# Scoring the heads of the second block's attention one at a time instead of in interleaved pairs

## The chip, the core and the metric

The kernel runs on one core of a Trainium2 chip. The metric is the device time of one execution in microseconds (us); several executions are timed and the median is taken. TensorE (PE in the profile) multiplies matrices, VectorE (DVE) and ScalarE (ACT) work on rows, GpSimd (POOL) and SyncE (SP) mostly issue DMAs.

## The reference

Two model blocks of two layers each on 512 tokens of width 1024, in float32. The change touches the attention of the second block. Layer 0 there is windowed attention with a sink, layer 1 global attention with normed queries and keys; both also look at 256 context tokens, and in layer 0 the context tokens attend to themselves.

```python
def _mixer_window(q, k, v, kc, vc, sink, cos, sin):
...
    def block(i):
...
        s_lat = jnp.einsum('bqhgd,bkhd->bhgqk', qb, kb).astype(jnp.float32)
        s_lat = jnp.where(mask, s_lat, NEG_INF_2)
        s_ctx = jnp.einsum('bqhgd,bkhd->bhgqk', qpb, kc).astype(jnp.float32)
        p_lat, p_ctx = _joint_softmax(s_lat, s_ctx, sink)
        return (jnp.einsum('bhgqk,bkhd->bqhgd', p_lat.astype(v.dtype), vb)
                + jnp.einsum('bhgqk,bkhd->bqhgd', p_ctx.astype(vc.dtype), vc))
```

There are 16 query heads of width 64, and blocks of 128 queries (four for the latent tokens, two for the context tokens). After attention come an output projection and a mixture of 32 experts, then the next layer.

## The kernel before

A plan of steps is written first (`make_plan`), and each engine then walks the same list of steps and issues its own part of each one in that order. Nothing reorders the steps later, so the place of a step in the plan is its place in every engine's queue.

The unit of attention work is one head (or, for context queries, two heads of different groups) for 128 queries. A unit has four steps:

- **scores** (PE, L1162): queries times keys into PSUM tile `SC`, which has two buffers (unit index modulo 2). A window or global head has two products: the "plain" one with the 256 context keys, and the "rotated" one with the latent keys (256 or 384 of them in the window layer, 512 in the global layer). Each contracts over only 64 rows. For an even head the plain product sits in the lower 64 rows of the array and the rotated one in the upper 64; for an odd head it is the other way round (`pieces`, L876). Window heads add one or two masks by a 128-row bf16 product with the identity (`SC<-KB`). The buffer must have been freed by the exp of the unit two before (`sc_free`). VectorE then takes a row minimum over the scores.
- **exp** (ACT, L1582): the exponentials from `SC` into `PR`; frees the `SC` buffer.
- **turn** (PE, L1567 is its ACT half): 128x128 transposes of `PR` into PSUM tile `TR` (two banks, four blocks in each), which ACT copies to `PT`. The profile's line is L1190.
- **weigh** (PE, L1192; its products are L1200): `PT` times the values into `PJ`; after four heads VectorE divides by the sums.

`attend_pair` (L236) orders these for two units at a time: scores of i and i+1, turn of i-2, exp of i, weigh of i-3, exp of i+1, turn of i-1, weigh of i-2. `o_turn` (L1308, products L1085) turns a finished block of 128 queries for the output projection. For a pair of window heads the masks of both come behind the four products of both. The loop at L474 to L476 calls `attend_pair` for 80 units in layer 0 (64 window heads, 16 context units) and 64 in layer 1; the first pair is begun ahead of the last projection tile (L452).

The attention of the first block (`attend`, L257) is already written head by head: scores of i, turn of i-2, exp of i, weigh of i-3.

Of the kernel before, what the change touches and what calls it, by code (L numbers as in the profile page):

```python
# [128 lines left out]
class Counting:  # L129
# [5 lines left out]
    def add(self, sem, n):  # L135
        self.count[sem.name] = self.count.get(sem.name, 0) + n
        self.latest = (sem, self.count[sem.name])
# [34 lines left out]
def make_plan(until=99):  # L172
# [24 lines left out]
    def add(kind, **kw):  # L197
        s = Step(kind=kind, tr_before=n["tr"] - len(kw.get("tr", ())), **kw)
        steps.append(s)
        users = kw.get("w")  # L200
        if users is not None and kw.get("last", True):

            for u, use in zip(users if isinstance(users, list) else [users], kw["pj"] if isinstance(kw["pj"], list) else [kw["pj"]]):
                u.done = use + 1
        return s

    def begin_unit(u, first):
        u.sc = take("sc")[0]
        u.index = attend.count
        attend.count += 1  # L210
        u.two_before = units_before[-2] if len(units_before) >= 2 else None
        units_before.append(u)
        n["mixed"] += u.kind == "diff"
        u.mixed = n["mixed"]
        u.first = first
        if u.slot == 0:
            attend.batch += 1
            n["sinks"] += u.kind in ("window", "ctx")
        u.batch, u.sinks = attend.batch, n["sinks"]
        s = add("scores", u=u)  # L220
        u.needs = s.tr_before

    def turn_unit(u):
        u.tr = take("tr", -(-u.blocks // 4))
        add("turn", u=u)

    def weigh_unit(u):
        if u.slot == 0:
            attend.pj = take("pj")[0]
        u.pj = attend.pj  # L230
        if not u.full:
            n["part"] += 1
        u.part = n["part"]
        add("weigh", u=u)

    def attend_pair(unit_list, i, after):  # L236


        m = len(unit_list)
        if i < m:  # L240
            begin_unit(unit_list[i], i == 0)
            begin_unit(unit_list[i + 1], False)
        if 2 <= i < m + 2:
            turn_unit(unit_list[i - 2])
        if i < m:
            add("exp", u=unit_list[i])
        if i - 5 in after:
            after[i - 5]()
        if 4 <= i < m + 4:
            weigh_unit(unit_list[i - 3])  # L250
        if i < m:
            add("exp", u=unit_list[i + 1])
        if 2 <= i < m + 2:
            turn_unit(unit_list[i - 1])
            weigh_unit(unit_list[i - 2])

    def attend(unit_list, extra=None, after=None):  # L257

# [37 lines left out]
    for l in range(DEPTH):  # L296
# [29 lines left out]
        for ci, name in enumerate(names):  # L326
            w = weight("w_in", l=l, cols=CHUNKS[name])
            for t in range(XT_TILES):
# [7 lines left out]
                if ci >= 2:  # L336
# [6 lines left out]
                    for tt in (1, 2, 3):  # L343
                        if topk_left[tt] and tt < ci - 1:
                            k = min(4 if ci < 5 else 2, topk_left[tt])
# [13 lines left out]
        unit_list = []  # L359
# [48 lines left out]
    for l in range(DEPTH):  # L408
# [9 lines left out]
        unit_list, last_unit = [], []  # L418
# [20 lines left out]
        after = {k: oturn(t) for t, k in enumerate(last_unit)}  # L439
# [99 lines left out]
        for k, (what, e) in enumerate(order):  # L539
# [3 lines left out]
            u = Step(kind=what, l=l, e=e, index=base + k, slot=slot, loads=slot_loads[slot], prev=prev_use)  # L543
# [121 lines left out]
def build(nc, ins, out, until=99, debug=None):  # L665
# [6 lines left out]
    with ctx:  # L672
# [161 lines left out]
        sc_full, sc_free = sem("sc_full"), sem("sc_free")  # L834
# [41 lines left out]
        def pieces(u):  # L876
            t = u.t
            q = slice(t * P, (t + 1) * P)
            lo, hi = slice(0, HD), slice(HD, P)
            if u.kind in ("window", "global"):  # L880
                g, at_, k = u.h // 4, u.lat[0] * P, len(u.lat) * P
                plain, rotated = (hi, lo) if u.h % 2 else (lo, hi)
                found = [(256, CTX, QS[plain, u.h, q], KCTX[plain, g, :]),
                         (512, k, QS[rotated, u.h, q], KROT[rotated, g, at_:at_ + k])]
                if plain == hi:
                    found.reverse()
                for k, kb in enumerate(u.lat):
                    if u.kind == "window" and kb != t:
                        found.append((512 + k * P, P, identB, belowB if kb < t else aboveB))
                return found  # L890
            ext = u.keys * P if u.kind != "ctx" else CTX
            found = []
            for m, half in enumerate((lo, hi)):
                if u.kind == "ctx":
                    g = u.h // 4
                    qc = slice((t - XT_TILES) * P, (t - XT_TILES + 1) * P)
                    found.append((512 * m, ext, QCTX[half, (g // 2) * 4 + u.h % 4, qc], KCTX[half, g + m, :]))
                elif u.kind == "diff":
                    found.append((512 * m, ext, blk[half, u.h, q], blk[half, 4 + u.h, 0:ext]))
                elif u.kind == "dsa":  # L900
                    found.append((512 * m, ext, blk[half, 14 + u.h // 2, q], blk[half, 13, 0:ext]))
                else:
                    found.append((512 * m, ext, blk[:, 16 + u.h + m, q], blk[:, 20 + u.h + m, 0:ext]))
            for m in range(2):
                if u.kind == "dsa" and t:
                    found.append((512 * m, ext, identB, SELt[t]))
                elif u.kind != "ctx":
                    found.append((512 * m + t * P, P, identB, aboveB))
            return found
# [156 lines left out]
        def _(pe):  # L1066
# [34 lines left out]
                           YR[g][0:CAP, h * 512:(h + 1) * 512], start=g == 0, stop=g == 1)  # L1101
                return x

            scored_units = {}

            def score(u, ps, a, b):

                for k, (col, n, lhsT, rhs) in list(enumerate(ps))[a:b]:
                    bank = col // 512
                    m = mm(SC[:, u.sc % 2, col:col + n], lhsT, rhs, start=all(p[0] // 512 != bank for p in ps[:k]),  # L1110
                           stop=all(p[0] // 512 != bank for p in ps[k + 1:]), skip_group_check=True)
                return m
# [6 lines left out]
            for s in steps:  # L1119
                if s.kind == "open":  # L1120
                    turn_open(s.t, s.tr)
                elif s.kind == "project":
# [6 lines left out]
                    for c in range(DC):  # L1129
                        if c == DC // 2 and s.inner:  # L1130
                            turn_open(s.t + 1, s.inner)
                        m = mm(bank[:, 0:n], XT1[:, c, s.t * P:(s.t + 1) * P], w[:, c, 0:n], start=c == 0,  # L1132
                               stop=c == DC - 1)
                    m.then_inc(pj_full, 1)
                elif s.kind == "stage_turn":
# [3 lines left out]
                    for k in range(s.count):  # L1139
                        m = turn(bank[0:s.rows, k * P:(k + 1) * P], STG[:, base + k * s.rows:base + (k + 1) * s.rows],  # L1140
                                 identF)
                    m.then_inc(tr_full, 1)
                elif s.kind == "forget":
# [4 lines left out]
                    for t in range(XT_TILES):  # L1148
                        for j in range(t + 1):
                            m = mm(bank[:, 4 * t:4 * t + 4], triF if j == t else onesF, FT[3][:, 4 * j:4 * j + 4],  # L1150
                                   start=j == 0, stop=j == t)
# [9 lines left out]
                    x.then_inc(sc_full, 1)  # L1161
                elif s.kind == "scores":  # L1162
                    u = s.u
                    scored_units[u.index] = u
                    if u.first:
                        pe.wait_ge(tr_free, u.needs)
                    if u.kind == "dsa" and u.t:
# [1 line left out]
                    if u.sc >= 2:  # L1169
                        pe.wait_ge(sc_free, u.sc - 1)  # L1170
                    ps = pieces(u)
                    if u.kind != "window":
                        score(u, ps, 0, len(ps)).then_inc(sc_full, 1)
                        continue

                    score(u, ps, 0, 2)
                    if u.h % 2:
                        for a in (scored_units[u.index - 1], u):
                            score(a, pieces(a), 2, 2 + len(a.lat) - 1).then_inc(sc_full, 1)
                elif s.kind == "turn":  # L1180
                    u = s.u
                    if u.kind == "diff":
# [4 lines left out]
                    for k, use in enumerate(u.tr):  # L1187
                        bank = tr_slot(use)
                        for b, src in enumerate(blocks[4 * k:4 * k + 4]):
                            m = turn(bank[:, b * P:(b + 1) * P], src, identF)  # L1190
                        m.then_inc(tr_full, 1)
                elif s.kind == "weigh":  # L1192
                    u = s.u
# [3 lines left out]
                    for col, n, vs in weighed(u):  # L1197
                        for b, v in enumerate(vs):
                            for r in range(0, P, HALF_ROWS):
                                m = mm(bank[r:r + HALF_ROWS, col:col + n], PT[:, o + r:o + r + HALF_ROWS], v, start=b == 0,  # L1200
                                       stop=b == len(vs) - 1)
# [5 lines left out]
                elif s.kind == "ada":  # L1207
# [5 lines left out]
                    for c in range(DC):  # L1213
                        for g in range(4):
                            m = mm(bank[32 * g:32 * g + 2, 0:P], SCT[:, 2 * c:2 * c + 2], w[:, c, g * P:(g + 1) * P],
                                   start=c == 0, stop=c == DC - 1)
# [18 lines left out]
                elif s.kind == "scored":  # L1235
# [6 lines left out]
                    for c in range(4):  # L1242
                        for h in range(2):
                            k = 4 * h + c
                            m = mm(SC[64 * h:64 * h + ROUTER, 0, 0:P], RWT[:, k * ROUTER:(k + 1) * ROUTER],
                                   xt2(s.t)[:, k, :], start=c == 0, stop=c == 3)
# [12 lines left out]
                elif s.kind == "ranks":  # L1259
                    pe.wait_ge(mask_ready, s.index + 1)  # L1260
                    pe.wait_ge(rank_read, s.index)
                    for j in range(s.t + 1):
                        m = mm(SC[:, 1, 0:EXPERTS], beforeB if j == s.t else onesB, MASKB[:, j * EXPERTS:(j + 1) * EXPERTS],
                               start=j == 0, stop=j == s.t)
                    m.then_inc(rank_full, 1)
                    if s.t == s.tiles - 1:
                        pe.wait_ge(rank_read, s.index + 1)
                        for j in range(s.tiles):
                            m = mm(SC[:, 1, 0:EXPERTS], onesB, MASKB[:, j * EXPERTS:(j + 1) * EXPERTS], start=j == 0,
                                   stop=j == s.t)  # L1270
                        m.then_inc(count_full, 1)
                elif s.kind == "slots":
                    pe.wait_ge(slot_ready, s.index + 1)
                    for k in range(2):
                        m = mm(SC[0:CAP, 1, 512:512 + EXPERTS], SLOT[s.index % 2][:, k, :], OWNT[:, s.t, k, :],  # L1275
                               start=s.t + k == 0, stop=s.t == s.tiles - 1 and k == 1)
                    m.then_inc(slots_done, 1)
                elif s.kind == "fin_turn":
                    f = s.f
                    pe.wait_ge(fin_done, f.q)  # L1280
                    k = f.fin % 2
# [1567 lines left out]
```

## Time and profile before

| what | value |
|---|---|
| median of 3 runs | 2901.52 us (2897.41 to 2903.01) |
| profiled execution, its own time | 2897.14 us |
| its span | 2895.3 us |
| mean granted TensorE clock | 0.988 |
| TensorE busy (matmul) | 2785.2 us, 96% of the span |
| VectorE, ScalarE, GpSimd busy | 1115.7, 760.8 and 235.4 us |
| DMA | 636.91 MB, mean 220 GB/s |
| the chain that ended last | PE 20% of the span, DVE 1%, the rest 0% |

All times below are microseconds from the start of the span. The second block's attention lies at about 1016 to 1196 (layer 0) and 2015 to 2195 (layer 1). TensorE's matmuls are pipelined, so the duration of one says less than the distance from one start to the next. A group's line, such as L1110 for scores, is the line in the code above.

### The profile page before, as it was taken

Reading aid. Unit: us, or ns where it says so; the run is one execution under the profiler, and the core shown is the slowest. Engines: PE = TensorE matmul, PEld = TensorE weight load, DVE = VectorE, ACT = ScalarE, POOL = GpSimd, SP = SyncE. Lnnn points to the kernel's source line nnn. Section 1 sums busy time; section 2 is a strip of 40 time slices with the busy share of each in tenths; the row PEclk is TensorE's granted clock in tenths of the full one; section 3 lists DMA queues with packets and bytes.
Section 4 is the critical chain, followed back from the end, with each engine's and each line's share of the span. In section 5 each row is a group of like instructions: output and inputs, shape, how many; then the busy total and the mean of one; then the engine's idle time right before and its main releaser. Section 6 shows DMA issues by size and latency. Waiting matters only on the chain. (4 is left out here: it accounts for less than half of the span.)

```text
span 2895.3 us, 64923 instructions
## 1 busy us (share of the span) xinstructions
PE 2785.2 (96%) x27109; PEld 1650.7 (57%) x27109; DVE 1115.7 (39%) x2681; ACT 760.8 (26%) x1599; POOL 235.4 (8%) x400
## 2 busy tenths in 40 slices
PE   8999999999989999999999999989999999999996
PEld 4544655444644467546666666634675566666663
DVE  2572643672643255453221212273443522222224
ACT  1211521102631167411111111153773111111111
POOL 3000011000020000011000000120000100110001
PEclk9999999999989999999999999999999999999998
DMA  7213733114734000347999999861003699999993
GB/s 270 80 58 111 271 119 114 59 58 148 261 103 145 29 2 2 139 174 269 399 401 401 398 401 402 340 244 67 2 2 132 261 396 398 402 403 399 400 398 142
DMA packets 149741, 636.91 MB, mean 220 GB/s; under 512 B 14336, under 2 KB 18528, under 8 KB 133200
## 3 DMA queue, kind: packets, MB, share of 16 engines
q1 hardware_dynamic: 114624, 517.59, 46.2%
q0 software_dynamic: 34960, 117.16, 11.7%
q8 instruction: 106, 1.74, 0.2%
q14 instruction: 51, 0.42, 0.0%
HBM read 582.70 MB, written 52.00 MB: 219 GB/s over the span
## 5 line engine op out<-in xcount | busy, mean ns | idle before, releaser
L1132 PE MATMUL PJ<-WR,XT 128*128 128x512 f32 (+2 forms) x1152 | 475.4, 569 | 5.4 <-ACT XT L140 2.8
L140 ACT ACTIVATE PT<-TR 128x512 f32<-128x512 f32 (+3 forms) x384 | 177.8, 493 | 866.3 <-PE TR L1361 730.5
L1132 PEld LDWEIGHTS PJ<-WR,XT 128*128 128x128 f32 x1152 | 215.6, 191 | 243.8 <-issue 215.9
L140 DVE TENSOR_TENSOR PR<-G 128x384 f32<-128x384 f32 x64 | 35.7, 559 | 736.2 <-ACT G L140 735.8
L1090 PE MATMUL PJ<-WR,XT 128*128 128x512 f32 x576 | 259.0, 606 | 1.8 <-ACT XT L140 1.4
L1341 PE MATMUL SC<-QK,XT 128*64 128x256 f32 x2112 | 242.5, 383 | 0.0
L140 DVE TENSOR_REDUCE SM<-SC 128x1 f32<-128x768 f32 (+6 forms) x208 | 173.7, 835 | 172.5 <-PE SC L1110 167.3
L1292 PE MATMUL PJ<-WR,XT 128*128 128x512 f32 x512 | 225.7, 593 | 1.0 <-issue 1.0
L1341 PE MATMUL SC<-WR,XT 128*64 128x256 f32 x1984 | 226.2, 381 | 0.0
L1341 PEld LDWEIGHTS SC<-QK,XT 128*64 128x64 f32 x2112 | 149.4, 138 | 85.4 <-issue 14.5
L140 ACT ACTIVATE PR<-SC,SM 128x256 f32<-128x256 f32 (+5 forms) x288 | 187.6, 669 | 31.5 <-DVE SM L140 15.3
L140 ACT ACTIVATE XT<-TR 128x384 f32<-128x384 f32 (+1 forms) x204 | 99.4, 526 | 338.8 <-PE TR L1327 241.4
L1090 PEld LDWEIGHTS PJ<-WR,XT 128*128 128x128 f32 x576 | 109.9, 195 | 132.6 <-issue 130.4
L1341 PEld LDWEIGHTS SC<-WR,XT 128*64 128x64 f32 x1984 | 139.8, 137 | 79.6 <-issue 12.3
L1200 PE MATMUL PJ<-V,PT 128*64 128x65 f32 (+1 forms) x3904 | 167.4, 231 | 1.4 <-ACT PT L140 1.4
L1110 PE MATMUL SC<-QK 64*128 64x512 f32 (+7 forms) x512 | 155.0, 512 | 1.9 <-ACT PR L140 1.7
L1200 PEld LDWEIGHTS PJ<-V,PT 128*64 128x64 f32 x3904 | 135.8, 137 | 36.0 <-issue 32.6
L1292 PEld LDWEIGHTS PJ<-WR,XT 128*128 128x128 f32 x512 | 94.6, 190 | 108.3 <-issue 108.3
L140 ACT ACTIVATE QK<-TR 128x512 f32<-128x512 f32 (+4 forms) x108 | 59.2, 563 | 367.9 <-PE TR L1140 272.7
L1190 PE MATMUL TR<-KF,PR 128*128 128x128 f32 x976 | 148.0, 281 | 7.3 <-DVE PR L140 4.0
L1351 PE MATMUL SC<-QK,XT 128*32 128x128 f32 x4224 | 127.9, 273 | 0.0
L140 DVE TENSOR_TENSOR XT<-PJ,BC 32x256 f32<-32x256 f32 (+1 forms) x192 | 98.0, 510 | 74.1 <-PE PJ L1374 56.2
(253 smaller groups left out, 3147.5 us busy)
## 6 DMA issues: line engine op xcount, KB each, us to landing
QK<-in_w_gate_dram SPq DMA_DIRECT2D x34, 2048.0 KB, 9.4
WR<-in_w_down_dram SPq DMA_DIRECT2D x34, 2048.0 KB, 15.6
QK<-in_w_up_dram SPq DMA_DIRECT2D x32, 2048.0 KB, 13.2
WR<-in_w_up_dram SPq DMA_DIRECT2D x32, 2048.0 KB, 14.3
WR<-in_w_gate_dram SPq DMA_DIRECT2D x30, 2048.0 KB, 9.5
QK<-in_w_down_dram SPq DMA_DIRECT2D x30, 2048.0 KB, 15.8
WR<-in_w_ada_dram SPq DMA_DIRECT2D x24, 2048.0 KB, 8.5
WR<-in_w_in_dram SPq DMA_DIRECT2D x14, 2048.0 KB, 8.0
```

Source lines behind the costliest of these rows:

```text
L140: return lambda *a, **k: Signal(make(*a, **k), self)
L1090: m = mm(dst[:, 0:n], rows[:, c, :], w[:, c, 0:n], start=c == 0, stop=c == DC - 1)
L1110: m = mm(SC[:, u.sc % 2, col:col + n], lhsT, rhs, start=all(p[0] // 512 != bank for p in ps[:k]), stop=all(p[0] // 512 != bank for p in ps ...
L1132: m = mm(bank[:, 0:n], XT1[:, c, s.t * P:(s.t + 1) * P], w[:, c, 0:n], start=c == 0, stop=c == DC - 1)
L1190: m = turn(bank[:, b * P:(b + 1) * P], src, identF)
L1200: m = mm(bank[r:r + HALF_ROWS, col:col + n], PT[:, o + r:o + r + HALF_ROWS], v, start=b == 0, stop=b == len(vs) - 1)
L1292: m = mm(bank, rows[:, c, :], w[:, c, :], start=c == 0, stop=c == DC - 1)
L1341: mm(bank[CAP_A * h:CAP_A * (h + 1), k * 512:k * 512 + 256], XET[par][:, c, 0:CAP_A], w[:, c, 256 * h:256 * (h + 1)], start=c == 0, stop=c ...
L1351: x = mm(bank[CAP_B * q:CAP_B * (q + 1), k * 512 + 256:k * 512 + 384], XET[par][:, c, CAP_A:CAP], w[:, c, P * q:P * (q + 1)], start=c == 0 ...
```

## The change

`attend_pair` now orders its two units one after the other, with the same four steps in the order that the first block uses: scores of k, turn of k-2, exp of k, weigh of k-3, and then the same for k+1. On TensorE, a window head's products and masks are issued together, where before the masks of a pair came behind the products of both heads. The diff is whole:

```diff
-        if i < m:
-            begin_unit(unit_list[i], i == 0)
-            begin_unit(unit_list[i + 1], False)
-        if 2 <= i < m + 2:
-            turn_unit(unit_list[i - 2])
-        if i < m:
-            add("exp", u=unit_list[i])
-        if i - 5 in after:
-            after[i - 5]()
-        if 4 <= i < m + 4:
-            weigh_unit(unit_list[i - 3])
-        if i < m:
-            add("exp", u=unit_list[i + 1])
-        if 2 <= i < m + 2:
-            turn_unit(unit_list[i - 1])
-            weigh_unit(unit_list[i - 2])
+        for k in (i, i + 1):
+            if k < m:
+                begin_unit(unit_list[k], k == 0)
+            if 2 <= k < m + 2:
+                turn_unit(unit_list[k - 2])
+            if k < m:
+                add("exp", u=unit_list[k])
+            if k - 5 in after:
+                after[k - 5]()
+            if 3 <= k < m + 3:
+                weigh_unit(unit_list[k - 3])
...
-            scored_units = {}
-
...
-                    scored_units[u.index] = u
...
-                    if u.kind != "window":
-                        score(u, ps, 0, len(ps)).then_inc(sc_full, 1)
-                        continue
-
-                    score(u, ps, 0, 2)
-                    if u.h % 2:
-                        for a in (scored_units[u.index - 1], u):
-                            score(a, pieces(a), 2, 2 + len(a.lat) - 1).then_inc(sc_full, 1)
+                    score(u, ps, 0, len(ps)).then_inc(sc_full, 1)
```

The number of instructions of each kind is the same; only their order changes, on PE, ACT and DVE. GpSimd's and SyncE's rows are the same as before.

TensorE in the global layer (layer 1), one pair of heads, before. `SC<-V,QK` is the plain product, `SC<-QK` the rotated one, `TR<-KF,PR` the turn of one head, `PJ<-V,PT` its weighing:

```order
L1110 MATMUL SC<-V,QK 128x256
L1110 MATMUL SC<-QK 128x512 x2
L1110 MATMUL SC<-V,QK 128x256
L1190 MATMUL TR<-KF,PR 128x128 x6
L1200 MATMUL PJ<-V,PT 64x65 x12
L1190 MATMUL TR<-KF,PR 128x128 x6
L1200 MATMUL PJ<-V,PT 64x65 x12
```

The same in the changed kernel:

```order
L1103 MATMUL SC<-V,QK 128x256
L1103 MATMUL SC<-QK 128x512
L1175 MATMUL TR<-KF,PR 128x128 x6
L1185 MATMUL PJ<-V,PT 64x65 x12
L1103 MATMUL SC<-QK 128x512
L1103 MATMUL SC<-V,QK 128x256
L1175 MATMUL TR<-KF,PR 128x128 x6
L1185 MATMUL PJ<-V,PT 64x65 x12
```

The second head's two products have moved from beside the first head's to behind the first turn and weighing.

TensorE in the window layer, a pair of heads of the second or third query tile, before:

```order
L1110 MATMUL SC<-V,QK 128x256
L1110 MATMUL SC<-QK 128x384 x2
L1110 MATMUL SC<-V,QK 128x256
L1110 MATMUL SC<-KB 128x128 x4
L1190 MATMUL TR<-KF,PR 128x128 x5
L1200 MATMUL PJ<-V,PT 64x65 x10
L1190 MATMUL TR<-KF,PR 128x128 x5
L1200 MATMUL PJ<-V,PT 64x65 x10
```

The same, changed, for its first head:

```order
L1103 MATMUL SC<-V,QK 128x256
L1103 MATMUL SC<-QK 128x384
L1103 MATMUL SC<-KB 128x128 x2
```

The four masks of the pair have been split, two behind each head's own products.

ScalarE in the global layer, the exps (`PR<-SC,SM`) and the copies of turned blocks (`PT<-TR`, 512 and 256 wide for one head), before:

```order
L140 ACTIVATE PR<-SC,SM 128x768 x2
L140 ACTIVATE PT<-TR 128x512
L140 ACTIVATE PT<-TR 128x256
L140 ACTIVATE PT<-TR 128x512
L140 ACTIVATE PT<-TR 128x256
L140 ACTIVATE PR<-SC,SM 128x768 x2
```

Changed:

```order
L140 ACTIVATE PT<-TR 128x512
L140 ACTIVATE PT<-TR 128x256
L140 ACTIVATE PR<-SC,SM 128x768
L140 ACTIVATE PT<-TR 128x512
L140 ACTIVATE PT<-TR 128x256
L140 ACTIVATE PR<-SC,SM 128x768
```

The copy of the second head's turned blocks now stands ahead of that pair's second exp.

## Rows read from the trace of the kernel before

**Rows 1.** Windows: stretch, length, busy by engine (instructions), clock, DMA share, GB/s.
```profile
1016.30:1190.00 173.70, 168.04 (x2168) 121.33 (x2168) 96.08 (x265) 121.59 (x240) 0.00 (x0) 1.00 0.01 2
2037.00:2042.00 5.00, 4.36 (x14) 1.74 (x14) 1.06 (x5) 4.12 (x7) 0.00 (x0) 0.70 0.00 0
2053.00:2190.00 137.00, 134.32 (x1863) 100.49 (x1861) 68.83 (x136) 104.29 (x169) 0.00 (x0) 1.00 0.01 2
```

**Rows 2.** Timeline (start, us, what), PE: one global pair, scores, turn, next pair.
```profile
2072.54 0.48 PE L1110 MATMUL SC<-V,QK 64*128 64x256 f32 x1
...
2074.08 0.87 PE L1190 MATMUL TR<-KF,PR 128*128 128x128 f32 x6
...
2077.39 0.48 PE L1110 MATMUL SC<-V,QK 64*128 64x256 f32 x1
```

**Rows 3.** Timeline, PE: single heads of the first block, scores, masks, turn.
```profile
305.26 0.70 PE L1110 MATMUL SC<-QK 64*128 64x256 f32 x4
305.90 0.28 PE L1110 MATMUL SC<-KB 128*128 128x128 bf16 x2
...
321.84 0.92 PE L1110 MATMUL SC<-QK 64*128 64x384 f32 x4
322.69 0.29 PE L1110 MATMUL SC<-KB 128*128 128x128 bf16 x2
...
348.61 1.13 PE L1110 MATMUL SC<-QK 64*128 64x512 f32 x4
349.67 0.29 PE L1110 MATMUL SC<-KB 128*128 128x128 bf16 x2
349.79 0.61 PE L1190 MATMUL TR<-KF,PR 128*128 128x128 f32 x4
```

**Rows 4.** Timeline, ACT and DVE in the pair of Rows 2: minimum, copy, exps.
```profile
2073.80 0.96 DVE L140 TENSOR_REDUCE SM<-SC 128x1 f32<-128x768 f32 x1 [2.51 <-PE SC L1110]
...
2074.86 0.87 ACT L140 ACTIVATE PT<-TR 128x512 f32<-128x512 f32 x2 [0.98 <-PE TR L1190]
...
2075.76 2.06 ACT L140 ACTIVATE PR<-SC,SM 128x768 f32<-128x768 f32 x2
```

**Rows 5.** Timeline, PE: one window pair of the second query tile, and the next.
```profile
1071.39 0.48 PE L1110 MATMUL SC<-V,QK 64*128 64x256 f32 x1
...
1072.90 0.72 PE L1190 MATMUL TR<-KF,PR 128*128 128x128 f32 x5
...
1073.55 0.80 PE L1200 MATMUL PJ<-V,PT 128*64 128x65 f32 x20
...
1074.37 0.74 PE L1190 MATMUL TR<-KF,PR 128*128 128x128 f32 x5
...
1075.77 0.48 PE L1110 MATMUL SC<-V,QK 64*128 64x256 f32 x1
```

**Rows 6.** Timeline, PE: a window pair of the first query tile, and the next.
```profile
1032.11 0.48 PE L1110 MATMUL SC<-V,QK 64*128 64x256 f32 x1
...
1033.47 0.60 PE L1190 MATMUL TR<-KF,PR 128*128 128x128 f32 x4
...
1035.82 0.48 PE L1110 MATMUL SC<-V,QK 64*128 64x256 f32 x1
```

**Rows 7.** Timeline, PE: a pair of context units, and the next.
```profile
1177.87 1.51 PE L1110 MATMUL SC<-V,QK 64*128 64x256 f32 x8
1179.32 0.66 PE L1190 MATMUL TR<-KF,PR 128*128 128x128 f32 x4
...
1181.72 1.51 PE L1110 MATMUL SC<-V,QK 64*128 64x256 f32 x8
```

**Rows 8.** Timeline, PE: waits (in brackets) at layer 1's start and end.
```profile
2037.50 0.48 PE L1110 MATMUL SC<-V,QK 64*128 64x256 f32 x1 [2.73 <-ACT PR L140]
...
2190.43 0.84 PE L1190 MATMUL TR<-KF,PR 128*128 128x128 f32 x6 [1.14 <-ACT PT L140]
```

**Rows 9.** Timeline, PE: sixteen passes of projection, 512 wide over all 128 rows.
```profile
1017.49 7.08 PE L1292 MATMUL PJ<-WR,XT 128*128 128x512 f32 x16
```

## The prediction, written before the changed kernel ran

> **What bounds the kernel now.** I read three views in this order. The windows first [rows 1]: in the global layer's attention TensorE is busy for 134.3 of 137.0 us, at a granted clock of 1.00, and ScalarE for 104.3; in the window layer it is 168.0 of 173.7, ScalarE 121.6. The DMA columns beside them say 2 GB/s, so no transfer runs under either stretch that could hide a longer or use a shorter attention. The time of these stages is what TensorE's instruction stream needs, plus the few waits in it. Then the timeline of TensorE, to see what its stream consists of: I take distances from one start to the next, since matmuls overlap. A global pair [rows 2] takes 2072.54 to 2077.39 = 4.85 us, of which the scores of both heads take 1.54 (to the first turn) and two turns and two weighings the other 3.31. Last the same view in the first block [rows 3], which orders heads one by one already, and so shows what a head scored alone costs.
>
> **What the rows say of a head scored alone.** A head's two products sit in different halves of the array and run at the same time. With both 256 wide, the scores last 305.90 - 305.26 = 0.64 us until the masks; with both 384 wide 0.85; with both 512 wide 1.06 [rows 3]. That is 0.21 for each further 128 columns of both, above some 0.22 that a group of scores costs once. A pair of global heads has 512 + 256 on either half, since the second head has its halves swapped: 0.22 + 6 x 0.21 = 1.48, and 1.54 is what is seen. Alone, a global head has 512 on one half and 256 on the other. If the longer half decides, that is 1.06 and two of them 2.12; if the halves shared one stream, the mean width of 384 would count, 0.85, and two 1.70. The trace has no row of unequal halves alone. What decides for me: a pass of 512 over all 128 rows takes 7.08 / 16 = 0.44 [rows 9], and the step from two 256-wide passes to two 512-wide ones in both halves at once costs 1.06 - 0.64 = 0.42, so 0.42 for 2 x 256 more columns on either side. A half in company is as fast as the full array by itself, so the companion takes nothing away and its absence gives nothing back. I take the longer half: 1.06. Upper end 1.10, since a 128-row float32 turn and not a bf16 mask follows here.
>
> The interleaving of before thus was a packing: the short product of one head ran beside the long one of the next. The change takes this away wherever the two products differ in width, and everywhere pays the 0.22 of a group twice per pair instead of once.
>
> **The change part by part**, all on TensorE's stream; counts are of pairs.
>
> (A) Global layer, steady part: 27 pairs start between 2053.19 and 2184.37, 23 with scores of 1.54 as in rows 2, and four of 1.49 that do not wait for an exp. Two solo heads are 2.12. 23 x 0.58 + 4 x 0.63 = +15.9. Turns and weighings are the same instructions (3.31), and the period should be 5.43.
>
> (B) Window layer, second and third tile: 16 pairs. Today 1.51 for scores with four masks [rows 5]. Alone: 0.85 for a 384-wide longer half, and 0.12 for two masks (349.79 - 349.67 [rows 3]) = 0.97, twice 1.94. 16 x 0.43 = +6.9; two of these pairs wait today, 1.68 and 1.99, which goes: -0.7. The first weighing lasts 0.82 there, with the turn ahead 1.47 in all, against 1.40 for the second turn and weighing: the next turn waits for its bank. With scores between, that goes: 16 x 0.07 = -1.1. Together +5.1, a period of 4.38 becoming 4.7.
>
> (C) Window layer, first and last tile: 16 pairs with both products 256 wide. Alone 0.64 + 0.06 for one mask = 0.70, twice 1.40. Today 1.36 [rows 6] where the second head waits for an exp, which is most pairs, and 1.19 where it does not; the mean of the 16 is 1.33. +1.1, and minus some 1.7 for waits before scores, before the first weighing and after a tile's o_turn: -0.6.
>
> (D) Context units: 8 pairs, equal widths. Today 1.45 [rows 7], alone 0.67 each (0.64 and 0.03 for the turn that follows; between 0.64 and the 0.72 that would leave it even). A period of 3.85 becomes 3.74; with two o_turns whose waits shrink by 0.2 each: -1.3.
>
> (E) Ends. In layer 1 a turn waits 1.14 for a bank because ACT does two exps before it copies [rows 8]; with the copy between them it goes: -1.1, and the like in layer 0: -1.1. At layer 1's start scores wait 2.73 for an exp that is late because the last projection tile and its rope sit on VectorE and ScalarE in front of it [rows 8]. I estimate from the order of the steps there that the exp will be ready 0.5 to 1 us sooner, and that a turn further on, which like that of 2190.43 waits about 1.14 for a bank, no longer does: -2.2 in all, the least certain term. The pair begun ahead of the last projection becomes 0.6 longer: +0.6. Sum -3.8.
>
> **Does the new order add a wait?** The longest loop is scores, minimum, exp, buffer free. In the global layer [rows 4]: the minimum takes 0.96, a pair of exps 2.06, so one about 1.0, the copy 0.87 beginning 0.78 after its turn's start. Counted from the turn in slot k: copy done at 1.65, exp k from 1.7 to 2.7; the next turn comes at 2.7, the scores that need this buffer at 2 x 2.72 - 1.06 = 4.4. Slack 1.7. ScalarE's copy and exp are 1.9 of a period of 2.7. The weighing needs a copy that is a whole slot old. VectorE's division after each fourth head now stands between two minima, and queues behind it the minimum of the next head; it needs about 1 us and the scores beside it last 1.06. I cost all this at nothing; its cover is the slack just counted.
>
> **A rule of the Trainium skill, weighed.** TensorE's stream changes between 64-row products, full 128-row ones and 64-column ones: today five such changes per pair, from now on six. What the sixth costs stands in the rows as part of the 0.22 and of the turns' 0.04 after it, and is counted. "TensorEngine Tiling (Array Packing)", Key Properties, of the Trainium skill says that changing the tiling mode drains the engine, and "TensorE: Matmul & The Clock Gate" of the Trainium skill, Single matmul latency, puts the drain at about 175 ns. By it, as an estimate, 72 pairs might pay up to 0.07 more than counted, +5 us; the steps between rows show about 0.1 after a group of scores and I stay with them.
>
> **Sum.** 15.9 + 5.1 - 0.6 - 1.3 - 3.8 = +15.3 us. Against the profiled execution's own 2897.14 (span 2895.3 and 1.8 around it) this is 2912.4. That execution lies 4.4 below the median of 2901.52, within the spread of 2897.41 to 2903.01; against the median it is 2916.8. Everything behind attention starts later by the same amount: the expert weights' first transfers are issued as the attention ends.
>
> **Rivals.**
> 1. *Halves share a stream* (solo global head 0.85, not 1.06): A becomes 27 x 0.17 = +4.5, B 16 x 0.22 less 1.8 = +1.7, the pair ahead -0.4 and the rest as before, in sum about +0.1: 2901.6, no change. Against it are rows 9 and 3 side by side, as above. 6%.
> 2. *Faster*: a head scored alone costs no more than half a pair, because the array takes up the next head's loads during the weighing ahead of it and the 0.22 vanishes with the longer half's surplus. Then A = 0, B = -1.8, C = -1.7, D and E as counted less 0.6: -9.2, so 2892. The sign turns when A and B together lose 15.3 us over their 43 pairs, 0.36 per pair or 0.18 per head: at a solo global head below 0.88. The first block's heads [rows 3], which have this very order, show 1.06. 3%.
> 3. *A new wait in each slot*: ScalarE comes late for the turn's bank or the exp, say 0.3 in each of the 54 steady global heads, +16: 2933. It needs ScalarE to be 1 us later than rows 4 make it. 5%.
> 4. *Part of the waits stays or more goes*: TensorE's clock fell to 0.70 in the 5 us after the wait of 2.73 [rows 1, 8]. If the wait shrinks enough for the clock to stay at 1.00, up to 2.4 us more are won at that place: 2914.4. If none of E comes, 2920.6. Both are in the forecast's own range.
>
> **How the numbers follow.** The forecast with its range of 2909 to 2923 has 86%; the bounds are E with or without, 1.10 in place of 1.06 (+2.2 in A) and 2 to 3 us of spread between medians. The range of 8 in 10 is 2908 to 2924. A difference of 0.2%, 5.8 us, is about what a measurement of this kernel can tell from no change. Slower by more: the forecast nearly whole and rival 3, 91%. Within: rival 1 and the forecast's lower tail, 6%. Faster by more: rival 2, 3%.
>
> **What would show it.** In the changed profile: global slots of 2.72 us (turn to turn) with scores of 1.06 from their first start to the turn; window slots of 2.36 in the middle tiles and 1.86 in the outer ones; no wait of TensorE for an exp in steady state, so that TensorE's matmul columns stay at 98% or more while the stage is longer; the global stage 16 us longer and the window and context stage 1 to 3. The prediction is wrong if the solo scores of unequal halves last under 0.95, if bracketed waits stand in each slot, or if the time behind attention shrinks by what attention grows.

## The result and the profile after

The changed kernel takes 2919.04 us (median, 2918.15 to 2919.48, 4 runs) beside 2899.47 for the kernel before (2896.93 to 2903.01, 4 runs). The ratio is 1.0061, 95% interval 1.0047 to 1.0076: slower by 0.5 to 0.8%. The forecast was 2916.8 us, with a range of 2908 to 2924.

The two attention stages, each from the start of its first scores to the start of its last `o_turn`, carry most of it. In the windows view (stretch, length, then busy time and instructions of PE, PEld, DVE, ACT, POOL, then granted clock, DMA share, GB/s), the kernel before:

```profile
1016.30:1196.32 180.02, 172.13 (x2242) 124.43 (x2241) 98.76 (x278) 125.00 (x247) 0.00 (x0) 1.00 0.01 3
2015.48:2195.52 180.04, 170.51 (x2234) 123.79 (x2233) 87.32 (x176) 132.04 (x212) 0.00 (x0) 0.99 0.01 2
```

and the changed one:

```profile
1018.06:1200.28 182.22, 177.78 (x2241) 119.78 (x2241) 98.74 (x278) 125.06 (x247) 0.00 (x0) 1.00 0.01 3
2024.23:2216.98 192.75, 186.83 (x2233) 118.44 (x2233) 87.34 (x176) 132.11 (x212) 0.00 (x0) 0.99 0.01 2
```

Layer 0 grew by 2.20 us, layer 1 by 12.71. VectorE and ScalarE did the same work in the same busy time; TensorE's busy time grew by 5.65 and 16.32 us with the same instructions. More of its time is a product running in one half of the array with nothing in the other.

This is a pair of global heads of the changed kernel, on PE, which answers to [rows 2]:

```profile
2099.89 0.48 PE L1103 MATMUL SC<-V,QK 64*128 64x256 f32 x1
2099.90 0.69 PE L1103 MATMUL SC<-QK 64*128 64x512 f32 x1
2100.21 0.38 PE L1103 MATMUL SC<-V,QK 64*128 64x256 f32 x1
2100.43 0.59 PE L1103 MATMUL SC<-QK 64*128 64x512 f32 x1
2100.95 0.87 PE L1175 MATMUL TR<-KF,PR 128*128 128x128 f32 x6
2101.76 0.92 PE L1185 MATMUL PJ<-V,PT 128*64 128x65 f32 x24
2102.61 0.69 PE L1103 MATMUL SC<-QK 64*128 64x512 f32 x1
...
2103.66 0.88 PE L1175 MATMUL TR<-KF,PR 128*128 128x128 f32 x6
2104.46 0.92 PE L1185 MATMUL PJ<-V,PT 128*64 128x65 f32 x24
2105.31 0.48 PE L1103 MATMUL SC<-V,QK 64*128 64x256 f32 x1
```

Scores last 1.06 and 1.05 from their first start to the turn, where the pair had 1.54; the pair's period is 5.42, where it was 4.85. Both products start at once. The short one issues its second pass at 2100.21, the long one at 2100.43, and from there the long one runs on without a companion. For the wide window heads, which answer to [rows 5]:

```profile
1080.59 0.59 PE L1103 MATMUL SC<-QK 64*128 64x384 f32 x1
...
1081.43 0.28 PE L1103 MATMUL SC<-KB 128*128 128x128 bf16 x2
1081.56 0.72 PE L1175 MATMUL TR<-KF,PR 128*128 128x128 f32 x5
1082.20 0.80 PE L1185 MATMUL PJ<-V,PT 128*64 128x65 f32 x20
1082.93 0.48 PE L1103 MATMUL SC<-V,QK 64*128 64x256 f32 x1
```

0.97 for scores and masks, and 2.34 for a head, so 4.69 for two against 4.38. For the context units, which answer to [rows 7], a head takes 1.84, two 3.68 against 3.85.

```profile
1163.28 0.70 PE L1103 MATMUL SC<-V,QK 64*128 64x256 f32 x4
1163.91 0.66 PE L1175 MATMUL TR<-KF,PR 128*128 128x128 f32 x4
1164.50 0.69 PE L1185 MATMUL PJ<-V,PT 128*64 128x65 f32 x16
1165.12 0.70 PE L1103 MATMUL SC<-V,QK 64*128 64x256 f32 x4
```

ScalarE and VectorE are in time. Counted from the turn at 2100.95, the copy begins 0.78 later and the exp ends 2.67 later (2102.63 + 0.99), which is 1.7 before the scores that need its buffer, at 2105.31:

```profile
2101.16 0.96 DVE L140 TENSOR_REDUCE SM<-SC 128x1 f32<-128x768 f32 x1 [1.57 <-PE SC L1103]
2101.73 0.87 ACT L140 ACTIVATE PT<-TR 128x512 f32<-128x512 f32 x2 [0.82 <-PE TR L1175]
...
2102.63 0.99 ACT L140 ACTIVATE PR<-SC,SM 128x768 f32<-128x768 f32 x1
```

At layer 1's start and end, which answer to [rows 8], the wait for the late exp is 2.15 where it was 2.73, and the turn near the end, which had waited 1.14, has no bracket any more:

```profile
2045.87 0.48 PE L1103 MATMUL SC<-V,QK 64*128 64x256 f32 x1 [2.15 <-ACT PR L140]
```
```profile
2211.71 0.87 PE L1175 MATMUL TR<-KF,PR 128*128 128x128 f32 x6
2212.51 0.92 PE L1185 MATMUL PJ<-V,PT 128*64 128x65 f32 x24
2213.55 0.85 PE L1175 MATMUL TR<-KF,PR 128*128 128x128 f32 x6
```

The stages make 14.9 us. Of the 22.4 us between the two profiled spans (2917.7 and 2895.3), 7.5 lie outside them; of the 19.6 between the medians, 4.7. The experiments ask what these are.

### The profile page after: what moved, and what is told of

Same layout as the page of the kernel before. It is cut to its first block and busy times, and to the rows that moved or that the text cites. A ratio compares the mean times of both kernels' runs of the same rounds, so it can differ in the third digit from the quotient of the medians.

```text
span 2917.7 us, 64835 instructions
## 1 busy us (share of the span) xinstructions
PE 2813.1 (96%) x27105; PEld 1643.2 (56%) x27109; DVE 1115.6 (38%) x2681; ACT 761.4 (26%) x1599; POOL 235.7 (8%) x400
## 5 line engine op out<-in xcount | busy, mean ns | idle before, releaser
L1103 PE MATMUL SC<-QK 64*128 64x512 f32 (+7 forms) x512 | 183.3, 519 | 1.4 <-ACT PR L140 1.4
L1175 PEld LDWEIGHTS TR<-KF,PR 128*128 128x128 f32 x976 | 104.3, 141 | 60.8 <-ACT PR L140 37.0
```

## The experiments

All ratios are to runs of the kernel before on the same chip, in the same job. The theory: the longer half of the array decides how long a head's scores last, and a pair was cheap since one head's short product ran beside the other's long one. The rivals: the halves share one stream; the order of waits, and not the packing, made the pair cheap; part of the loss lies outside attention.

### E1, the short product twice, heads one by one

```diff
+                    if u.kind == "global":
+                        ps = [p for p in ps for _ in range(1 + (p[0] == 256))]
```

(with start and stop set for each product of a global head, so that the second one overwrites the first).

> The changed kernel, but each global head multiplies its short product (plain, 256 wide) twice into the same place; 64 heads do 256 columns more on one half of the array. Theory (the longer half of the array alone sets a head's scores, and the short one runs beside it for nothing): both halves now carry 512, scores stay at 1.06 us, layer 1 and the whole stay within 1 us of the changed kernel (about +19 us against before). Rival (the halves share a stream, the sum of widths counts): 0.21 us more per head, 64 x 0.21 = +13 us, about +33 against before.

2913.58 us, ratio 1.0054 (1.0032 to 1.0076). Two heads on PE:

```profile
2100.61 0.69 PE L1103 MATMUL SC<-QK 64*128 64x512 f32 x1
2100.62 0.70 PE L1103 MATMUL SC<-V,QK 64*128 64x256 f32 x2
2101.14 0.59 PE L1103 MATMUL SC<-QK 64*128 64x512 f32 x1
2101.15 0.59 PE L1103 MATMUL SC<-V,QK 64*128 64x256 f32 x2
2101.68 0.87 PE L1177 MATMUL TR<-KF,PR 128*128 128x128 f32 x6
...
2103.33 0.48 PE L1103 MATMUL SC<-V,QK 64*128 64x256 f32 x1
```

Four passes of 256 beside two of 512 take 1.07 where two beside two took 1.05 to 1.06. Layer 1's stage is 193.7 us against 192.75. 64 more products cost 0.9 us, not 13, and 0.44 of it falls on the one pair that still stands side by side, ahead of the last projection (9.87 us to the next scores, where it was 9.43). A head scored alone has that much room in its shorter half. The halves do not share a stream.

### E2, the same in the pairs of before

The same two lines in the kernel before.

> The kernel before, pairs as they were, with the short product of each global head multiplied twice. Theory: in a pair each half carries 256 + 512 now and 256 x 2 + 512 then, so the pair's scores grow from 1.54 to about 1.90 (0.22 + 8 x 0.21), 32 pairs x 0.37 to 0.42 = +12 to +13 us against before. Rival (a pair was cheap because of the order of waits and not because the long product ran beside the other head's short one): under +4 us.

2909.39 us, ratio 1.0038 (1.0026 to 1.0049). One pair:

```profile
2101.55 0.48 PE L1110 MATMUL SC<-V,QK 64*128 64x256 f32 x1
2101.57 0.69 PE L1110 MATMUL SC<-QK 64*128 64x512 f32 x1
...
2103.48 0.88 PE L1192 MATMUL TR<-KF,PR 128*128 128x128 f32 x6
```

Scores 1.93 instead of 1.54, layer 1's stage 191.7 instead of 180.0, so +11.6 us for the same 64 products that cost 0.9 in E1. And with both halves full, heads one by one (193.7) are only 2.0 us behind pairs (191.7), where with unequal halves they are 12.7 behind. So of the 12.7 us some 10.7 are the empty half beside the long product. The other 2.0 are the group of scores that is begun twice, 5.0 over the 26 steady pairs (146.5 against 141.5), less 2.1 at the layer's start and 0.8 at its end, where waits go.

### E3 and E4, the new order in one layer alone

`attend_pair` takes the new order where `u.l == 0` (E3) or `u.l == 1` (E4), and the old one elsewhere; the masks of window heads go with it.

> Head by head in the window layer (layer 0) only, pairs in the global layer. Theory from the two traces: the stage of layer 0 from its first scores to its last o_turn grows by 2.2 us (180.0 to 182.2), layer 1 stays at 180.0; in all +2 us against before, or +2 to +9 if what the changed kernel lost outside both stages (about 7 us between the two profiles) hangs on layer 0. Rival (that outside part is only variation between executions): stages as said and the outside part the same as before, within 3 us.

> Head by head in the global layer (layer 1) only. Theory: the stage of layer 1 grows by 12.7 us (180.0 to 192.8), layer 0 stays at 180.0; in all +13 us against before. Rival (the outside part follows the longer layer 1): +17 to +20 us.

E3: 2900.43 us, ratio 1.0013 (1.0002 to 1.0023); stages 182.22 and 180.07. E4: 2909.49 us, ratio 1.0043 (1.0033 to 1.0054); stages 180.03 and 194.29. The two layers add up but for 1.5 us, by which layer 1 of E4 lies above that of the changed kernel. This excess lies at its start, and by these rows the clock accounts for it. In the changed kernel the granted clock falls right behind the wait of 2.15, to a mean of 0.66 over five microseconds, and the next scores still wait 0.89 for an exp, so that part of what the slow clock costs would have been a wait in any case. In E4 it is 1.00 behind the first wait (2.14), TensorE then waits 0.67 and 1.73, and only behind that does it fall, where no wait follows that could hide it:

```profile
2047.03:2052.03 5.00, 5.00 (x38) 3.26 (x38) 1.12 (x2) 3.73 (x6) 0.00 (x0) 0.66 0.01 3
```

The same piece of layer 1, from the start of its second pair of heads to that of its sixth, lasts 26.58 us in the changed kernel, 28.12 in E4, and 26.61 in E1, where the clock does not fall at all. The outside part is 2535.4 and 2532.6 us: it follows neither layer.

### E5, the changed kernel again

> The changed kernel as it is, a second time. In its first profile 7.5 us more than in the profile of before lay outside the two attention stages (2542.7 against 2535.2), while four other kernels with one or both stages changed show 2532.6 to 2537.1 there. Theory (the outside part is variation between executions and chips): stages 182.2 and 192 to 194 again, outside 2532 to 2540, ratio to before about 1.0051 (+15 us). Rival (the changed order brings something about outside the stages): outside 2542 again, ratio 1.0065 or more.

2918.54 us (2912.08 to 2921.47), before 2901.71 (2893.39 to 2906.91), ratio 1.0057 (1.0039 to 1.0075). Stages 182.22 and 192.74, outside 2538.5. The stages repeat to 0.01 us. The outside part does not: over the two first profiles and the eight of the experiments it is 2532.6 to 2542.7 us, and the kernel before alone spreads over 13 us in one job. The 4.7 us between the first medians are within that; the ratio is a little above what the stages give (1.0051), and 16.8 us against 14.9 is no difference that these runs can settle.

### E6, the pairs of before with each head's masks behind its own products

```diff
-                    if u.kind != "window":
+                    if True:
```

> The order of before (pairs), but a window head's masks are issued right behind its own products and not behind those of both heads. Theory (a full 128-row mask between the heads ends the packing): in the 16 pairs with 384-wide products the scores grow from 1.51 to 1.94 us, +6.9; in the others (256 wide) from 1.19 to 1.40 where nothing waits and hardly at all where the second head waits for an exp, +1; layer 0's stage about 187 to 188 us against 180.0, more than the 182.2 of the changed kernel because the waits of the pair order stay; layer 1 stays at 180; +7 us. Rival (masks run between for their own 0.06 us each): under +1 us.

2915.35 us, ratio 1.0048 (1.0030 to 1.0065). One pair of the second tile:

```profile
1075.08 0.48 PE L1110 MATMUL SC<-V,QK 64*128 64x256 f32 x1
...
1075.92 0.28 PE L1110 MATMUL SC<-KB 128*128 128x128 bf16 x2
1076.14 0.59 PE L1110 MATMUL SC<-QK 64*128 64x384 f32 x1
...
1076.98 0.28 PE L1110 MATMUL SC<-KB 128*128 128x128 bf16 x2
1077.10 0.72 PE L1190 MATMUL TR<-KF,PR 128*128 128x128 f32 x5
```

Nothing in TensorE's queue moved but two masks of 0.06 us, and the pair's scores grew from 1.51 to 2.02. The second head's products start only behind both masks, 0.22 after the first of them, and have the array to themselves. Layer 0's stage is 189.7 us, 9.7 more than before, and 2 more than I had expected: a return from masks to half-array products costs 0.09 in each pair (1.49 against twice 0.70, 2.03 against twice 0.97), which heads one by one do not pay, since a weighing stands in front. It is shown with this that ending the packing costs layer 0 that much when nothing else moves; the changed kernel's +2.2 is this loss, less the 0.09 per pair and less the waits that the old order had. Layer 1, which the edit does not touch, was expected to stay at 180 and took 181.4. The difference is again at its start (29.66 us for the piece that takes 28.28 before), where the granted clock falls twice in this run, to 0.67 behind a wait of 2.74 and to 0.71 over the five microseconds from 2059.14; before it falls once.

### E7, pairs, but the copy of turned blocks ahead of the second exp

```diff
-        if i < m:
-            add("exp", u=unit_list[i + 1])
         if 2 <= i < m + 2:
             turn_unit(unit_list[i - 1])
+        if i < m:
+            add("exp", u=unit_list[i + 1])
+        if 2 <= i < m + 2:
             weigh_unit(unit_list[i - 2])
```

> Pairs scored side by side as before, but on ScalarE the copy of the second head's turned blocks stands ahead of the pair's second exp, as in the changed kernel. The packing stays. Theory (this order suits only heads that are scored apart; the scores of the next pair's second head now wait for a later exp): the second head's scores wait about 0.5 us in each global pair and 0.4 in each window pair, layer 1 +10 to +15, layer 0 +8 to +12, in all +18 to +27 us. Rival (the order of copies and exps does not matter in steady state and only helps the ends): -1 to -2 us.

2946.94 us, ratio 1.0160 (1.0137 to 1.0183), stages 202.2 and 202.3: +22 in each, twice what I had expected. The pair on PE and ACT:

```profile
2099.97 0.69 PE L1111 MATMUL SC<-QK 64*128 64x512 f32 x1 [0.26 <-ACT PR L140]
...
2102.68 0.87 PE L1191 MATMUL TR<-KF,PR 128*128 128x128 f32 x6
2102.71 0.99 ACT L140 ACTIVATE PR<-SC,SM 128x768 f32<-128x768 f32 x1
...
2103.78 0.87 ACT L140 ACTIVATE PT<-TR 128x512 f32<-128x512 f32 x2
...
2104.34 0.69 PE L1111 MATMUL SC<-QK 64*128 64x512 f32 x1
...
2104.69 0.99 ACT L140 ACTIVATE PR<-SC,SM 128x768 f32<-128x768 f32 x1
...
2105.73 0.69 PE L1111 MATMUL SC<-QK 64*128 64x512 f32 x1 [0.27 <-ACT PR L140]
```

It closes a loop: the second head's scores (2099.97), two turns, the copy held back by the first exp (2103.78), the second exp (to 2105.68), and the buffer for the next pair's second head: 5.76 us per pair. I had only set the later exp against the old period, and had not followed its delay around. I had also expected the packing to stay, and it does not: the first head's scores begin at 2104.34 and the second's only at 2105.73, 1.39 later, when the first's are done (a head alone takes 1.06). The pair's scores last 2.45 instead of 1.54, and these 0.91 are the whole growth of the period (5.76 against 4.85); only some 0.3 of them are the wait itself. The order of waits thus matters very much to pairs, and of the two the old one is right for them; it is not what the change lost by, for in the changed kernel nothing waits for an exp in steady state.

### E8, each order where it is cheaper

```diff
+    def single(u, i, m):
+
+        return u.kind == "ctx" or u.kind == "window" and u.t == 0 or u.kind == "global" and i < 10
```

Units that it names go head by head, the others as pairs; in the last pair of all the second exp stands behind the copy.

> Each order where it is cheaper: head by head for the first window tile, for the context units and for the first ten global heads; pairs for the wide window tiles and the other global heads; in the last global pair the copy ahead of the second exp. From the segments of the two traces: layer 0 -0.2 (first tile), -1.4 (context units), -0.8 (end) = 177.6 us against 180.0; layer 1 -1.7 (start), -1.0 (end) = 177.3 against 180.0; in all -5 us, ratio 0.9982. Rival (the seams between the orders cost what the parts gain): -2 to +1 us.

2898.93 us, ratio 0.9994 (0.9983 to 1.0004): no difference that can be measured in the whole. In the trace the stages are shorter by 1.7 and 2.1:

```profile
1021.65:1199.99 178.34, 173.25 (x2241) 123.67 (x2241) 98.80 (x278) 125.01 (x247) 0.00 (x0) 1.00 0.01 3
2018.45:2196.37 177.92, 171.54 (x2234) 123.82 (x2233) 87.36 (x176) 132.04 (x212) 0.00 (x0) 0.99 0.01 2
```

3.8 of the 5 us expected; the rest went at the seams, where the first pair behind single heads has scores of 2.12 instead of 1.68, and at the end of layer 1, where one weighing still lasts 1.20 and the turn after it waits 0.28.

## Why the prediction was right, point by point

| term | forecast | in the trace |
|---|---|---|
| A, global layer, 27 pairs | +15.9 | +14.9 for 26 pairs, and 0.6 for the last: +15.4 |
| B, window tiles 2 and 3 | +5.1 | +4.4 (73.72 to 78.10) |
| C, window tiles 1 and 4 | -0.6 | 0.0 (+0.3, -0.5 and +0.2) |
| D, context units | -1.3 | -1.4 (33.74 to 32.38) |
| E, ends and layer 1's start | -3.8 | -3.6 |
| sum | +15.3 | +14.9 |

**The disputed step**, whether the longer half or the sum of both decides, was settled as forecast: 1.06 and 1.05 in the trace, and E1 and E2 show the mechanism by itself. The reasoning from [rows 3] and [rows 9], that a companion takes nothing away, held. Rival 1 falls with E1, rival 2 with the scores themselves. Rival 3 falls with the waits view: in the steady part of layer 1 TensorE waits for ScalarE three times 0.6 us, ahead of the `o_turn`s, in both kernels, and not in each slot. This is the changed one, 2060 to 2210:

```profile
PE TR L1080 <- ACT PT L140: 1.9, 3, 0.6
```

**A** was 0.5 high. Half of it is the first weighing after an `o_turn`, which fell from 0.94 to 0.85 three times and which I had counted as unchanged; the other half is that the second head of a pair takes 1.05 and not 1.06. **B** was 0.7 high. A turn and weighing of a wide head now last 1.37 to 1.38 us, where I had counted 1.40: the second turn of a pair, which stood behind a weighing, took 0.67 to the weighing after it, and behind a mask it takes 0.64 or 0.65. Over 32 heads that is the 0.7. **C** had the gain 0.6 too large. The wait of 0.41 for an exp in the first tile, which I had counted as going, is still there as 0.45:

```profile
1044.15 0.48 PE L1110 MATMUL SC<-V,QK 64*128 64x256 f32 x1 [0.41 <-ACT PR L140]
```
```profile
1046.03 0.48 PE L1103 MATMUL SC<-V,QK 64*128 64x256 f32 x1 [0.45 <-ACT PR L140]
```

The first pair of the layer, whose products the first head's mask now parts, costs 0.3 and not 0.2.

**E** is right in sum by errors that cancel. The pair ahead of the last projection was to cost 0.6 and cost nothing. The new loop puts no turn between units 0 and 1 of layer 1, so they still stand side by side and pack; from their scores to the next scores it is 9.43 us in both kernels. That this term and the overstated savings cancel is luck. Layer 1's start gave 1.7 of the 2.2 forecast (0.6 of the late exp, and the 1.14 of a turn), its end 1.0 of 1.1, layer 0's end 0.8 of 1.1.

**Rival 4** put a price of up to 2.4 us on the fall of the clock at layer 1's start. In the changed kernel the clock was not spared: it is 0.74 in the five microseconds from 2045, as it was 0.70 in those from 2037 before [rows 1], and 0.66 in both when counted from the end of the wait.

```profile
2045.00:2050.00 5.00, 4.13 (x36) 2.89 (x38) 1.47 (x4) 4.65 (x7) 0.00 (x0) 0.74 0.00 0
```

In E1 it was spared, behind a wait as long:

```profile
2043.73 0.48 PE L1103 MATMUL SC<-V,QK 64*128 64x256 f32 x1 [2.12 <-ACT PR L140]
```
```profile
2043.73:2048.73 5.00, 4.35 (x47) 3.31 (x48) 1.38 (x5) 4.34 (x7) 0.00 (x0) 1.00 0.00 0
```

And nothing was won by it: that piece of the layer takes 26.61 us in E1 and 26.58 in the changed kernel, since the faster TensorE waits 0.65 for a copy and 1.73 for the next exp instead of 0.89. No run bears out the 2.4.

**The rule of the skill.** The further 5 us did not come: the steady parts A and B stayed below their forecasts, which went by [rows 3]. E6 gives a size for one return from a full-array bf16 mask to half-array products, 0.09 us. "TensorEngine Tiling (Array Packing)", Key Properties, of the Trainium skill says that changing the tiling mode drains the engine; what part of the 0.09 is such a drain no run here tells. "TensorE: Matmul & The Clock Gate" of the Trainium skill, Single matmul latency, gives about 175 ns for the drain, as part of the latency of a single matmul and not as the cost of a change of mode; what E6 measured is about half of it.

**The whole** came out 2 us above the forecast, 2919.0 against 2916.8, and the second time at +16.8. The stages explain 14.9; what lies above is of the size of what varies outside them.

## What to carry to other kernels

Where products contract over only half the array, put those side by side whose summed widths fill both halves equally. In these runs the cost of a group is its longer half, and a full-array instruction between two such products ends the group, even a mask of 0.06 us (E6). An order of steps on one engine fits only its partner's order on the other: before a copy and an exp change places, follow the delay once around the loop of buffers. When a change moves 0.5%, measure its stages from first start to last start in the trace; they repeated to 0.01 us while the whole varied by ten. Look at the granted clock there too: where it fell at another place, a stage moved by 1.4 or 1.5 us without any change of its order (E4, E6).

## What I had not expected of the hardware

A second 256-wide float32 product beside a 512-wide one costs 0.01 to 0.02 us (1.07 against 1.05 to 1.06). Coming back from a full-array mask to half-array products costs 0.09 us, which heads one by one, with a weighing in front, do not pay a second time. Waits of nearly the same length had different effects on the clock: behind 2.15 us in the changed kernel the granted clock was 0.66 over the next five microseconds, behind 2.12 in E1, 2.65 in E2 and 2.14 in E4 it was 1.00. What decides between them these runs do not show.
